# The recurrent queries and keys are projected by feature, from tokens that also come laid out by feature

## The reference, cut to what matters

```python
h = rms_norm(x, g_mix)
p = h @ w_in                         # columns: attention q, k, v; recurrent q, k, v; output gate; gates
aq, ak, av, mq, mk, mv, mo, mi, mf = split(p)
att = sliding_window_attention(rms_norm(aq), rms_norm(ak), av)
qk = silu(causal_dwconv(concat([mq, mk]), conv_qk))   # 4 taps along the tokens, 512 features
mh = sigmoid(mo) * mlstm_chunkwise(*split(qk), mv, gates)
x = x + concat([rms_norm(att), rms_norm(mh)]) @ w_out
x = x + (silu(rms_norm(x) @ w_gate) * (rms_norm(x) @ w_up)) @ w_down
```

## Time and profile before

| what | value |
|---|---|
| median of 3 runs | 1007.28 us (1007.04 to 1007.73) |
| the profiled execution | 1006.92 us, its span 1005.2 us |
| busy in the span | TensorE 998.6 us, GpSimd 692.1, VectorE 648.3, ScalarE 438.1 |
| moved by DMA | 66.00 MB, mean 66 GB/s |
| unit 8 starts | 62.07 us from the span's start |
| unit 16 starts | 85.86 us from the span's start |

### The profile page before, as it was taken

How to read it: one execution, slowest core, us unless ns; L and a number is a source line. 1 busy time by engine, 2 the same in 40 slices (tenths; PEclk the granted TensorE clock), 3 DMA queues, 4 the chain that set the end, 5 groups by cost and what they waited for, 6 DMA issues and landing times.

```text
span 1005.2 us, 13420 instructions
## 1 busy us (share of the span) xinstructions
PE 998.6 (99%) x4960; PEld 830.7 (83%) x4960; DVE 648.3 (64%) x777; ACT 438.1 (44%) x904; POOL 692.1 (69%) x545
## 2 busy tenths in 40 slices
PE   8999999999999999999999999999999999999998
PEld 7899888888888888888888888888888888888887
DVE  4259526558862678885748577674748586674585
ACT  7545145547750657524334352433334252433440
POOL 0128768826675515996887787887878788788792
PEclk9999999999999999999999999999999999999999
DMA  7113212141032002112112112112112212211213
GB/s 240 59 53 93 64 44 69 59 157 33 22 126 64 21 11 74 53 42 84 43 42 84 42 42 81 46 42 75 52 43 67 61 42 57 70 42 48 83 59 137
DMA packets 71017, 66.00 MB, mean 66 GB/s; under 512 B 5288, under 2 KB 53544, under 8 KB 70952
## 3 DMA queue, kind: packets, MB, share of 16 engines
q1 hardware_dynamic: 69944, 64.64, 20.8%
q10 hardware_dynamic: 1008, 0.50, 0.2%
HBM read 60.42 MB, written 4.21 MB: 64 GB/s over the span
## 4 chain that ended last, share of the span: by engine, by line
PE 96%; DVE 2%; ACT 1%; issue 1%; DMA 0%; SPq 0%; DVEq 0%; ACTq 0%
PE banks L812 30%; PE banks L814 29%; PE banks L813 29%; PE banks L832 1%; PE banks L1008 1%; PE banks L905 1%; PE banks L983 1%; ACT prob L1511 1%; PE banks L970 1%; PE banks L917 0%; DMA x_in<-in_x 0%; PE banks L927 0%; PE banks L881 0%; PE banks L870 0%; DVE af_lo_apart L2069 0%
## 5 line engine op out<-in xcount | busy, mean ns | idle before, releaser
L742 POOL TENSOR_TENSOR wr_lo<-wr_raw,wr_hi 128x512 fp32r<-128x512 f32 x231 | 319.3, 1414 | 26.8 <-ACT wr_hi L1329 21.6
L736 POOL TENSOR_TENSOR wr_raw<-wr_raw,wr_raw 128x512 f32<-128x512 f32 x132 | 193.3, 1469 | 132.5 <-PE banks L814 75.8
L812 PE MATMUL banks<-hf_hi,wr_hi 128*128 128x512 f32 x616 | 239.9, 390 | 0.0
L814 PE MATMUL banks<-hf_hi,wr_lo 128*128 128x512 f32 x616 | 239.7, 389 | 0.0
L813 PE MATMUL banks<-hf_lo,wr_hi 128*128 128x512 f32 x616 | 239.7, 389 | 0.0
L1329 ACT ACTIVATE wr_hi<-wr_raw 128x512 fp32r<-128x512 f32 x231 | 136.7, 625 | 164.8 <-POOL wr_raw L736 107.5
L2151 DVE TENSOR_TENSOR x<-banks,x 128x1024 f32<-128x1024 f32 x138 | 168.8, 1224 | 51.6 <-PE banks L814 35.2
L812 PE MATMUL banks<-w_hi,actT_hi 128*128 128x512 f32 (+1 forms) x448 | 173.1, 386 | 0.0
L814 PE MATMUL banks<-w_hi,actT_lo 128*128 128x512 f32 (+1 forms) x448 | 168.4, 376 | 0.0
L813 PE MATMUL banks<-w_lo,actT_hi 128*128 128x512 f32 (+1 forms) x448 | 168.2, 375 | 0.0
L812 PEld LDWEIGHTS banks<-hf_hi,wr_hi 128*128 128x128 f32 x616 | 115.6, 188 | 24.4 <-issue 0.3
(11 more groups left out here) (204 smaller groups left out, 1191.3 us busy)
## 6 DMA issues: line engine op xcount, KB each, us to landing
wr_raw<-in_w_up SPq DMA_DIRECT2D x46, 256.0 KB, 3.2
wr_raw<-in_w_gate SPq DMA_DIRECT2D x44, 256.0 KB, 3.3
wr_raw<-in_w_down SPq DMA_DIRECT2D x44, 256.0 KB, 3.2
w_raw<-in_w_in SPq DMA_DIRECT2D x32, 256.0 KB, 3.3
w_raw<-in_w_out SPq DMA_DIRECT2D x16, 256.0 KB, 2.6
x<-in_x SPq DMA_DIRECT2D x8, 512.0 KB, 6.5
out<-x SPq DMA_DIRECT2D x16, 256.0 KB, 2.1
x_in<-in_x SPq DMA_DIRECT2D x7, 512.0 KB, 4.4
```

What stands on the lines that cost most here:

```text
L736: nc.gpsimd.tensor_tensor(wr_raw[slot(q, f)][:, :], wr_raw[slot(q, a)][:, :], wr_raw[slot(q, b)][:, :], ALU.subtract).then_inc(wsum, 1)
L742: nc.gpsimd.tensor_tensor(wr_lo[s][:, :], wr_raw[s][:, :], wr_hi[s][:, :].bitcast(F32), ALU.subtract).then_inc(wf_lo, 1)
L812: nc.tensor.matmul(ps, x_hi, wh, start=first, stop=False, skip_group_check=more)
L814: return nc.tensor.matmul(ps, x_lo, wh, start=False, stop=last, skip_group_check=more)
```

## The change

x is given to the kernel a second time, laid out by feature (`x_by_feature`, 1024 features by 1024 tokens), and the gains are given as one array of 128 rows by 34 columns, loaded by one transfer.

- The transposes of x and of the products of group 0 are gone, and `mqraw` with them. `xf_raw` (in the place of `actT_lo`) is loaded by half of the tokens and feature block; ScalarE rounds it to `actT_hi` (`feature_high`), VectorE subtracts in place (`feature_low`).
- Group 0 has weights as the stationary side and 512 tokens as the moving side. `recurrent_first_half` goes through k, four accumulators (banks 0 to 3) at once; `recurrent_second_half` goes through the four feature blocks f one after the other (banks 4 to 7).
- The products come out with features on partitions, so `rstd` must lie along a row: SP stores the `rstd` of a half to DRAM and loads it back spread over all partitions (`spread_rstd`, `r_bc`), after weight block 1 for the first half and after block 3 for the second. x tiles 4 to 7 are loaded after the first.
- VectorE multiplies by `r_bc` on reading out (`recurrent_rows`), and `convolution(half, f)` runs on 512 tokens.
- `keep_warm(9)` at the start in the place of 4 and 2.

```diff
+            def spread_rstd(half):
+                sp.wait_ge(rstd_ready, 4 * half + 4)
+                sp.dma_start(r_dram[4 * half:4 * half + 4, :].rearrange("t p -> p t"),
+                             rstd[:, 4 * half:4 * half + 4],
+                             allow_slow_non_contiguous=True).then_inc(r_stored, 16)
+                sp.wait_ge(r_stored, 16 * (half + 1))
+                for t in range(4 * half, 4 * half + 4):
+                    sp.dma_start(r_bc[:, t * P:(t + 1) * P],
+                                 r_dram[t:t + 1, :].to_broadcast([P, P])).then_inc(r_bc_s[half], 16)
+            for k in range(K):
+                load_features(0, k)
                 sp.dma_start(w0_raw[:, k, :], w_in_k[k, :, MQ:MQ + N]).then_inc(w0_s[k], 16)
+            for t in range(4):
+                load_x(t)
+            sp.wait_ge(w0_hi, K)
+            for k in range(K):
+                load_features(1, k)
...
-                if xt < T:
-                    load_x(xt)
-                    xt += 1
+                if n == 1:
+                    spread_rstd(0)
+                    for t in range(4, T):
+                        load_x(t)
+                if n == 3:
+                    spread_rstd(1)
...
+            def recurrent_first_half():
+                for k in range(K):
+                    pe.wait_ge(xf_hi, k + 1)
+                    pe.wait_ge(w0_hi, k + 1)
+                    for f in range(4):
+                        nc.tensor.matmul(bank[f][:, :], w_hi[:, k, f * P:(f + 1) * P], actT_hi[:, 0, k, :],
+                                         start=k == 0, stop=False)
+                    pe.wait_ge(xf_lo, k + 1)
+                    for f in range(4):
+                        nc.tensor.matmul(bank[f][:, :], w_hi[:, k, f * P:(f + 1) * P], actT_lo[:, 0, k, :],
+                                         start=False, stop=False)
+                    pe.wait_ge(w0_ready, k + 1)
+                    for f in range(4):
+                        last = nc.tensor.matmul(bank[f][:, :], w_lo[:, k, f * P:(f + 1) * P], actT_hi[:, 0, k, :],
+                                                start=False, stop=k == K - 1)
+            def recurrent_second_half():
+                for f in range(4):
+                    c = slice(f * P, (f + 1) * P)
+                    for k in range(K):
+                        if f == 0:
+                            pe.wait_ge(xf_lo, K + k + 1)
+                        last = three(bank[4 + f][:, :], w_hi[:, k, c], w_lo[:, k, c], actT_hi[:, 1, k, :],
+                                     actT_lo[:, 1, k, :], k == 0, k == K - 1)
+                    last.then_inc(mq_done, 1)
...
+            for k in range(K):
+                feature_high(0, k)
+                if k == 0:
+                    act.wait_ge(cols_s, 16)
                 w0_high(k)
+            for t in range(4):
+                stats(t)
+            for k in range(K):
+                feature_high(1, k)
+            for n in range(4):
+                w_scale(n)
+                stats(4 + n)
+            for n in range(4, K):
+                w_scale(n)
+            act.wait_ge(mq_done, 8)
+            w_scale(K)
...
+            def recurrent_rows(half, f):
+                dve.wait_ge(mq_done, 4 * half + f + 1)
+                if f == 0:
+                    dve.wait_ge(r_bc_s[half], 16 * 4)
+                V_.tensor_tensor(rawT[:, f, 3 + half * H:3 + (half + 1) * H], bank[4 * half + f][:, :],
+                                 r_bc[:, half * H:(half + 1) * H], ALU.mult).then_inc(mq_evac, 1)
...
+            for f in range(4):
+                recurrent_rows(0, f)
+            for f in range(4):
+                convolution(0, f)
+            for f in range(4):
+                recurrent_rows(1, f)
+                convolution(1, f)
```

More of the change, by code:

```diff
@@ L71, in constants, with columns, hymba_block @@
     return c
-def hymba_block(nc, x, g_mix, w_in, b_gates, conv_qk, q_gain, k_gain, sinks,
-                g_att, g_ml, w_out, g_ffn, w_gate, w_up, w_down, consts, out):
+def columns(g_mix, conv_qk, q_norm_gain, k_norm_gain, g_attn_out, g_mlstm_out):
+    rows = [conv_qk[0].reshape(-1, P), g_attn_out.reshape(-1, P), g_mlstm_out.reshape(-1, P),
+            np.tile(k_norm_gain, 2), np.tile(q_norm_gain, 2), g_mix.reshape(-1, P)]
+    return np.ascontiguousarray(np.concatenate(rows, axis=0).T)
+def hymba_block(nc, x, x_f, gains, w_in, b_gates, sinks, w_out, g_ffn, w_gate, w_up, w_down, consts, out):
     S, D = x.shape[1], x.shape[2]
@@ L206, in hymba_block @@
         E = v_end
[L207 to L216, removed]
         qkT, e = place("qkT", [P, 4, S], at=E)
+        x_in = [place(f"x_in{i}", [P, D], at=e + 4 * D * i)[0] for i in range(4)]
         mvx, e = place("mvx", [P, T, MH, DV + 1], at=e)
@@ L280, in hymba_block @@
         raw_s = [sem(f"raw_loaded{i}") for i in range(RAW)]
-        w0_s = [sem(f"w0_loaded{i}") for i in range(K)]
+        w0_s = [sem(f"w0_and_features_loaded{i}") for i in range(K)]
         x1_s = [sem(f"x1_loaded{i}") for i in range(2)]
@@ L1033, in out_unit @@
                     last.then_inc(done, 1)
+            WARM = 9
             def keep_warm(n):
@@ L1040, in _ @@
             pe.wait_ge(ones_set, 1)
[L1041 to L1047, removed]
+            keep_warm(WARM)
+            recurrent_first_half()
+            recurrent_second_half()
+            for U in range(T, ALL):
                 g, t = U // T, U % T
@@ L1406, in state_squares @@
                 act.wait_ge(ssb_done, t + 1)
-            for U in range(ALL):
+            for U in range(T, ALL):
                 g, t = U // T, U % T
@@ L1729, in _ @@
             step(V_.memset(mm[:, 0, :], 0.0))
[L1730 to L1744 removed]
+            dve.wait_ge(cols_s, 16)
@@ new lines, in _ @@
+            for k in range(K):
+                feature_low(0, k)
+                w0_low(k)
+            V_.tensor_scalar(cols[:, G_Q:G_Q + 1], cols[:, G_Q:G_Q + 1], HD ** -0.5, None,
+                             ALU.mult).then_inc(cols_ready, 1)
+            dve.wait_ge(par_s, 16 * PARAMS)
+            for i2 in range(2):
+                rows = slice(i2 * CHUNK, (i2 + 1) * CHUNK)
+                heads = sinks8[rows, :].rearrange("p (g b i) -> p g b i", g=KV, i=2)[:, :, :, i2]
+                link(V_.tensor_copy(sink_b[rows, :].rearrange("p (g c b) -> p g c b", g=KV, c=2),
+                                    heads.unsqueeze(2).to_broadcast([CHUNK, KV, 2, 2])))
@@ L2191 @@
     nc = bacc.Bacc("TRN2", target_bir_lowering=False, num_devices=1, dynamic_dma_scratch_size=1024)
+    laid = dict(inputs)
+    laid["x_by_feature"] = np.asarray(inputs["x"])[0].T
+    laid["gains"] = columns(*[np.asarray(inputs[name]) for name in GAINS])
     arrays, args = {}, []
     for name in NAMES:
-        a = np.ascontiguousarray(inputs[name])
+        a = np.ascontiguousarray(laid[name])
         arrays[f"in_{name}"] = a
```

224 lines of the change are left out of this document (70 added, 154 removed).

## The result

The changed kernel is slower than before: 1014.73 us median of 4 runs (1013.87 to 1016.95) against 1007.32 (1007.04 to 1007.73), a ratio of 1.0078 with the interval 1.0066 to 1.0090. The forecast was 998.7, with a range to 1003.4. The profiled execution took 1015.28 us, its span 1013.5.

A forecast was written before the change was run, and what follows sets the result against it. TensorE's stream, busy 99% of the span, was taken as the bound; unit 16 starting at 77.3 instead of 85.86 gave 8.6 us, so 1007.28 - 8.6 = 998.7 us, with an 8-in-10 range of 994.4 to 1003.4.

The forecast's parts named there:

- the price of the small stores: Storing each half's 512 factors to DRAM on SP's queue: 2.5 us in quiet, plus 2.0 behind queued bytes for the first.
- Both ends of the bound, 1.4 and 4.7: Limits for a small store's price: 1.4 us, the small row table's store; 4.7, the moved values in 448 pieces.
- S: Time at which SP reaches weight block 4, after the second store and its four spreads: forecast 46.6 us.
- ScalarE's chain: From x tile 4's landing at 33.1: four row sums, three weight blocks and 0.2 of waiting, ending at 42.5.
- Unit 16: Landmark on TensorE's timeline, after which its stream is unchanged: start forecast at 77.3 instead of 85.86, a gain of 8.6.
- Block 6: Weight block for TensorE's unit 8, issued when block 4 is ready: forecast ready at S + 8.8 = 55.4.
- a rival with 0.2: TensorE, idle 3.2 us after 52.2, drops to 1.2 GHz for half of unit 9: 1.2 us more, 999.9; chance 0.2.
- The small stores are dear: Factor stores cost more: 1003.6 at 4.7 each, 1007.9 at 180 ns a packet; chance 0.1 for 1002 to 1006, 0.04 slower.
- The full gain (994.6): Rival: weights come in time, S under 42.4, units 8 and 9 don't stop, gain 12.7 us; chance 0.12.
- The new order of matmuls: Rival: bank changes slow group 0's matmuls; 0.26 instead of 0.228 costs 6.1 us, giving 1000.7; chance 0.04.
- the stop in unit 8: TensorE held at k = 6 from about 52.2 to 55.4, waiting for GpSimd's split of a weight block.
- the start costs nothing: At TensorE's start, 1 us lost would cost nothing in the end, since everything after unit 8 hangs on S.

The follow-up runs named there:

- experiment 1: Changed kernel with each factor store writing four dense 512-byte rows of ones, factors left out of the result: 1000.83 us, ratio 0.9933 to the kernel before.
- experiment 8: Changed kernel with the 512 single 4-byte elements per store each in its own 512 bytes, factors left out: 1002.83 us, ratio 0.9960.
- experiment 4: Changed kernel with factors spread by diagonal and TensorE, no DRAM trip; x tiles 4 to 7 and the parameter wait moved: 995.40 us, ratio 0.9878.
- experiment 7: Changed kernel with the scattered stores issued from ScalarE's queue, SP loading meanwhile and reading back later: 1004.35 us, ratio 0.9966.
- experiment 3: Changed kernel with only SP's order changed: x tiles 4 to 7 before the first store, second store and read-back behind later weight blocks: 1007.75 us, ratio 1.0005.
- 11: experiment 4 plus one scattered store of 512 elements behind weight block 3 that nobody waits for until the end: 995.64 us, ratio 0.9883.

## Why the prediction was wrong

**The step that failed** is the price of the small stores: "I take 2.5 in quiet, and 2.0 behind the queue", reached through 36 ns a packet. The two took 8.25 and 8.08 (experiment 1 in their place 2.19 and 1.16). The first landed 6 us after the queued bytes had run out, where the forecast had 2.0. Both ends of the bound, 1.4 and 4.7, were of transfers whose pieces are rows, and the way to the price, packets by time per packet, could not have found it: the second store's packets end within 1.3 us of its issue.

**How S moved by 13.2.** First store landed at 33.26 for 28.0, +5.3 (fifteen issues of SP took 8.1 from 16.84 for the forecast's 6 from 15.8, so it went out 2.6 late; the bytes ahead of it ran to about 27, forecast 26.0); four spreads +0.4; x tile 4 landed 5.4 after its issue for 3.5, +1.9; ScalarE's chain -0.2; second store 8.1 for 2.5, +5.6; spreads +0.2. Experiment 1 gives 46.10 for the forecast's 46.6, but that it comes so near is in part luck: x tile 4 took the same 1.9 longer there, and the cheap stores landed 1.3 before (26.69 for 28.0) and 1.3 faster (1.16 for 2.5) than forecast. The path through SP's queue, x tile 4 and ScalarE was right; of its terms the stores were far off and the landing of tile 4 (5.4 for 3.5) by 1.9.

**Behind S, 3.7 more.** Unit 16 came at S + 34.4 for S + 30.7. Block 6 was ready at S + 10.9 for S + 8.8: the first landing took 3.1 for 2.2 and GpSimd's subtraction 1.23 for the 0.75 of the earlier trace rows in both rounds, which is 1.9 of the 2.1. And the clock fell, which was a rival with 0.2, not part of the forecast. Windows of the changed kernel (length, five engines busy, granted clock, DMA):

```profile
58.90:65.60 6.70, 0.34 (x3) 0.14 (x2) 2.48 (x4) 1.73 (x4) 1.21 (x2) 0.73 0.28 81
65.70:76.00 10.30, 7.23 (x29) 6.31 (x30) 9.94 (x14) 4.57 (x9) 4.75 (x4) 0.52 0.31 77
76.00:94.00 18.00, 18.00 (x152) 18.00 (x152) 3.72 (x6) 13.67 (x22) 8.46 (x8) 1.00 0.33 90
```

Idle for 6.4 us, TensorE came back at the 1.2 GHz level: matmuls of 264 columns 0.22 apart until 75.5, then 0.12. From 70.66 to unit 16 it took 23.5 us: 174 matmuls at 0.12 are 20.9, the lower clock made it 2.3 more and the wait for block 7 another 0.3. The forecast had 21.9 for this stretch, with 0.6 of waits and slack and 0.3 from taking 0.122 for 0.120. The difference is 1.6. With the 2.1 of block 6 that makes 3.7, and with S 16.9; the medians stand 0.9 nearer than the profiled executions, which leaves the 16.0. In experiment 1 waits of 2.4 and 0.56 us were enough: the three matmuls between them still ran at the upper level, those behind 57.42 at 0.22 until 60.2, which cost 1.4 us, where the rival had 1.2. These 1.4, and block 7 ready 1.2 later than forecast (57.42 for 56.2), less 0.2 of slack and 0.3 for the rounder 0.122, are the 2.1 us that remain of the miss there (unit 16 at 79.37 for 77.3). The Trainium skill ("TensorE: Matmul & The Clock Gate", Part 1) has the clock fall after idle time; the windows agree.

**The rivals.** "The small stores are dear" is what happened, on its slower side, which had 0.04. Its point (4.3 us more per store) was passed: the landings were 5.3 and 5.6 further on than forecast. Its mechanism was wrong, though: it priced a packet at 170 ns, and the same packets at other addresses landed after 2.1 us in all (experiment 8). The full gain (994.6) is about what the change is worth without the trip and the early wait for the parameters: 995.40 in experiment 4, which pays 1.6 for its own matmuls. The new order of matmuls isn't slower: 0.91 for four in the first half, 0.227 each as before.

**A wait that I had costed at nothing.** The load of `sinks` is one of the parameters ahead of the store on the queue, issued at 21.48, 3.5 us before it; it landed after 10.9 us (5.9 in experiment 1, where only the stores differ). So the dear store also holds back transfers that were issued before it. VectorE waits for it ahead of the low parts of the second half, and TensorE stopped 5.25 us at 33.67:

```profile
32.45 0.37 DVE L1732 COPY sink_b<-sinks 64x8 f32<-64x8 f32 x2 [14.79 <-DMA sinks<-in_attn_sinks]
```

That stop costs nothing in the sum, since the one in unit 8 follows it. In experiment 7 it is the largest that is left, 5.4 us.

**Confirmed.** First product at 5.50 (forecast 6.0), first half's end 28.4 (27.9), the stop in unit 8 from weights issued behind the second store. The forecast that the start costs nothing held as well, until experiment 4 took S off the path: there five warming calls are worth 2.5 us (2.8 by the ratios).

**Open.** Why elements that touch are dear. The 6.8 us between the last packet and the landing, and that other transfers are held back meanwhile, would suit writes to the same few bytes that wait for one another in memory, but no run shows memory's side. Between 4 and 16 bytes apart nothing was tried, nor a store of 128 side by side with no other near it, so how the price goes with number and distance is open.

## What to carry to other kernels

Before costing a small store by bytes or packets, look at where its elements land: two stores of 512 single elements laid out side by side in DRAM took 8 us each and held back the other transfers, and cutting one into four made it no better. If a per-token factor must lie along a row, spreading it with a diagonal and a matmul by ones costs 0.8 us per 512 tokens and leaves the DMA alone. And where a queue waits for a transfer, ask first what stands behind it: here two waits of 8 us on the loads' queue came out one to one in the end time.

## What the runs showed of the hardware

- Issue to landing in the quiet second half: 512 single elements side by side 8.1 us; 128 side by side 5.7 to 7.0, with others of their kind in flight; 128 at 16 bytes 2.6; 128 at 64 or 512 bytes 1.4; 512 at 512 bytes 2.1; 128 pieces of 16 bytes side by side 1.4; four rows of 512 bytes 1.2.
- The Trainium skill ("DMA: Bandwidth & Descriptors", Specifications) says that below 512 B the engines read, modify and write. The runs give it no price of its own here: 4-byte writes 64 bytes apart landed in 1.4 us.
- Loads of 128 KB issued from 0.1 us before to 4.3 us after a dear store took 7.3 to 9.7 us, whether SP or ScalarE had issued the store; without one the first of them takes 5.3 (experiment 1), the later ones 2.2 to 3.8. Those issued after it landed 1.3 to 3.0 us after the store itself had (experiments 3, 7, 11). They don't stand still meanwhile: in experiment 3 the engines moved 0.15 MB from 53.6 to 58.0, where the store landed, at 33 GB/s. With nothing behind the second store, in the changed kernel, they idled for 6.8 us. Loads issued up to 4.9 us ahead of the first store are late as well: the last block of x by feature (20.05) took 9.8 us for 6.8 in experiment 1, `sinks` 10.9 for 5.9.
- After a warming of 2.1 us and a pause of 2.3 us TensorE's matmuls ran at the 1.2 GHz level from 5.54 to 10.80; after one of 4.2 us and a pause of 0.1 they were at 2.4 GHz after 1.9 us.
